# Expert blocks of a mixture-of-experts stage: projection ahead of the transposes, and a gather without a bound

## The reference

```
dest = pad_starts[sorted_e] + (arange(NK) - starts[sorted_e])   # NK = 2048 tokens * 2 experts each
row_tok = full((cap,), N).at[dest].set(flat_tok[order])          # padding rows point past the tokens
def expert_block(rows, e):                                       # 128 rows, one expert
    xb = t_pad[rows]                                             # 128 x 1024
    hid = silu(xb @ w_gate[e]) * (xb @ w_up[e])                  # 128 x 256
    return hid @ w_down[e]                                       # 128 x 1024
y = zeros((N + 1, D)).at[row_tok].add(y_rows * row_w)
```

## Time and profile before

| | us |
|---|---|
| median of 3 runs | 3779.98 |
| lowest and highest run | 3773.37, 3782.13 |
| the profiled execution, its own time | 3773.37 |
| its span, first to last instruction | 3771.6 |
| first gather of the expert stage | at 3156.08 |
| last scatter issued | at 3761.32 |

### The profile page before, as it was taken

One profiled execution on the slowest core, in us unless ns is written; L12 is line 12 of the kernel. 1 busy time (PEld: TensorE's weight loads), 2 busy tenths in 40 slices (PEclk: granted clock), 3 DMA queues, 4 the chain that ended last, 5 costly groups with the idle time before them and its releaser, 6 DMA issues. The chain is left out here.

```text
span 3771.6 us, 33286 instructions
## 1 busy us (share of the span) xinstructions
PE 3512.1 (93%) x11453; PEld 1842.2 (49%) x11453; DVE 1708.3 (45%) x4081; ACT 1037.4 (28%) x2543; POOL 986.2 (26%) x1362
## 2 busy tenths in 40 slices
PE   4999999999999899989999997999999996999998
PEld 3754455555445544434444444555565554444443
DVE  4656623443364573326665556543443543222222
ACT  3122222211100460002235445533322221222222
POOL 0277767400000681000000004655530000221221
PEclk8999999999999999999999998999999997999999
DMA  3134445434254002222221000000112224999997
GB/s 136 58 127 144 155 145 165 144 114 133 94 166 141 34 12 112 90 89 77 69 96 34 23 14 4 1 1 1 68 36 84 86 82 178 310 334 331 332 335 236
DMA packets 115563, 451.57 MB, mean 120 GB/s; under 512 B 15635, under 2 KB 43155, under 8 KB 103356
## 3 DMA queue, kind: packets, MB, share of 16 engines
q1 hardware_dynamic: 91484, 370.18, 27.6%
q0 software_dynamic: 18432, 58.74, 5.8%
q10 hardware_dynamic: 5472, 20.45, 1.5%
HBM read 340.28 MB, written 117.42 MB: 121 GB/s over the span
## 5 line engine op out<-in xcount | busy, mean ns | idle before, releaser
L142 PE MATMUL pst<-arena 128*128 128x512 f32 (+5 forms) x6938 | 2757.5, 555 | 68.9 <-DMA arena<-in_w_exp 28.2
L142 PEld LDWEIGHTS pst<-arena 128*128 128x128 f32 x6938 | 1301.5, 198 | 1368.5 <-issue 1260.0
L164 POOL TENSOR_TENSOR arena<-arena 128x4 f32<-128x4 f32 (+7 forms) x784 | 409.2, 522 | 464.0 <-DVE arena L2024 403.6
L164 DVE TENSOR_TENSOR arena<-arena 128x1 f32<-128x1 f32 (+8 forms) x1260 | 457.8, 364 | 95.4 <-ACT arena L2254 20.2
L147 PE MATMUL pst<-arena 128*128 128x128 f32 x2145 | 329.0, 288 | 141.9 <-DVE arena L246 52.4
L147 PEld LDWEIGHTS pst<-arena 128*128 128x128 f32 x2145 | 258.9, 147 | 324.2 <-issue 166.3
L1286 POOL TENSOR_SCALAR arena<-arena 128x384 f32<-128x384 f32 (+1 forms) x128 | 151.7, 1202 | 563.9 <-DVE arena L1278 563.9
L153 ACT ACTIVATE arena<-pst,arena 128x128 f32<-128x128 f32 (+1 forms) x630 | 243.9, 482 | 104.6 <-PE pst L147 102.1
L2201 POOL TENSOR_SCALAR arena<-arena 128x512 f32<-128x512 f32 (+3 forms) x160 | 218.3, 1383 | 174.9 <-DVE arena L164 158.6
L167 DVE TENSOR_SCALAR arena<-arena 128x1 f32<-128x1 f32 (+11 forms) x581 | 140.9, 242 | 190.1 <-DMA arena<-in_bc 78.5
L173 ACT ACTIVATE arena<-arena 128x1024 f32<-128x1024 f32 x48 | 50.7, 1057 | 628.0 <-DVE arena L1522 371.6
(11 more groups left out here) (194 smaller groups left out, 2112.5 us busy)
## 6 DMA issues: line engine op xcount, KB each, us to landing
arena<-in_w_exp SPq DMA_DIRECT2D x48, 3072.0 KB, 11.9
arena<-in_w_ada SPq DMA_DIRECT2D x48, 512.0 KB, 4.7
rotd<-arena POOLq DMA_DIRECT2D x32, 512.0 KB, 4.0
arena<-rotd SPq DMA_DIRECT2D x32, 512.0 KB, 4.5
arena<-sgd SPq DMA_DIRECT2D x16, 1024.0 KB, 7.7
arena<-pwd SPq DMA_DIRECT2D x32, 416.0 KB, 5.5
pwd<-arena SPq DMA_DIRECT2D x16, 576.0 KB, 5.9
h2d<-arena SPq DMA_DIRECT2D x17, 512.0 KB, 2.9
```

The source lines that it names most:

```text
L142: x = t.do.matmul(o, l, r, start=(i == 0), stop=(i == len(pairs) - 1))
L164: own(v, s).tensor_tensor(o, a, b, op).then_inc(*inc(s, *event))
```

## The change

Three edits, all in the expert stage.

1. The gather loses its bound, so every row is fetched, the padding rows too.
2. On TensorE `te_moe_up(b)` moves ahead of `te_moe_hidden(b - 1)`.
3. On VectorE `ve_moe_hidden` goes away and its copy becomes the first operation of `ve_moe_down`, so it moves behind `ve_moe_up(b)`.

```diff
@@ po_moe_gather @@
             p.do.indirect_dma_start(out=xr[b % 3], out_offset=None, in_=h2d,
-                                    in_offset=bass.IndirectOffsetOnAxis(ap=idT[:, b:b + 1], axis=0),
-                                    bounds_check=S - 1, oob_is_err=False
+                                    in_offset=bass.IndirectOffsetOnAxis(ap=idT[:, b:b + 1], axis=0)
                                     ).then_inc(*dma(f"moe_xr{b % 3}", "xr", b))
@@
-        def ve_moe_hidden(v, b):
+        def ve_moe_down(v, b):
+            q = "moe_ve"
             v.wait_ge(*at("moe_pe", "hT", b))
             v.wait_ge(*at("moe_pe", "down", b - 2, 1))
-            vcopy(v, hTt[b % 2].rearrange("p a b -> p (a b)"), bank(4)[:, 0:256]).then_inc(*inc("moe_ve", "hT", b))
-
-        def ve_moe_down(v, b):
-            q = "moe_ve"
+            vcopy(v, hTt[b % 2].rearrange("p a b -> p (a b)"), bank(4)[:, 0:256]).then_inc(*inc(q, "hT", b))
             y_stored(v, b - 2)
@@ te_moe_run @@
             for b in range(lo, hi + 1):
+                if b < hi:
+                    te_moe_up(t, b)
                 if b > lo:
                     te_moe_hidden(t, b - 1)
-                if b < hi:
-                    te_moe_up(t, b)
                 if b + 1 < hi:
                     te_moe_turn(t, b + 1)
@@ ve_moe_run @@
             for b in range(lo, hi + 1):
-                if b > lo:
-                    ve_moe_hidden(v, b - 1)
                 if b < hi:
                     ve_moe_up(v, b)
```

## The result

The changed kernel takes 3802.64 us, the median of five runs (3799.89 to 3806.53), against 3779.98 us before. The ratio is 1.0072, 95% interval 1.0051 to 1.0092, so it is slower by some 27 us by the ratio and by 23 us by the medians. One more execution of the changed kernel is on record, at 3817.81 us, above all of the five. The forecast was 3813 us in a range of 3794 to 3830. The profiled execution took 3799.97 us with a span of 3798.2, 26.6 us more than the span before.

The account below looks back on a forecast made before the run. Two bounds: a two-block loop of load latency plus `up` to `down`, 12.26 us a block, and TensorE's pace, 11.40. Terms 1.29 + 27.1 + 4.4 = 32.8 us, gather 0, gave 3812.8 on the median's scale, forecast 3813, range 3794 to 3830.

Parts of the forecast that it names:

- The copy behind the two multiplies delays each `down`: Expert stage, VectorE: the copy waits for tanh and two multiplies, so each `down` ends 1.29 us later after its `up`.
- The loop through the load is the pace, TensorE's own pace the floor: Expert stage: load-to-`down` loop over two blocks grows 23.99 to 25.28 us; TensorE's own pace 11.40 to 12.5 a block.
- The relief of loads that land sooner: Weight loads: landing down to 10.4 us in the longer period, loop stops binding; +14 us, 3794; chance 0.14.
- The wait for the copy: Sign in the steady stretch: TensorE waits for the L158 copy some 45 times, near 1.0 us each, 40 us or more.
- The half clock: Rival, TensorE: stalls plus weight waits slow `up` by 3 us in every third block; 48 us more, 3860; chance 0.03.
- The sum was 32.8 us: Whole expert stage: first `down` 1.29, 21 loop turns 27.1, three crossings and last block 4.4 us; loads unchanged.
- crossings: Places where the chain passes over a block whose `up` had its weights in time; each priced 1.1 us at TensorE's pace.
- 20 turns of the loop, without their loads: Load, `up`, `turn`, `down`, next load, spanning two blocks: each turn 1.29 us longer; the prediction priced 21 turns, 27.1 us.
- both ends of the stage: Expert stage's start and end: first `down` 1.29 us later, last block 1.1 us more at TensorE's pace, last loop turn 1.29.
- the upper bound of 8.9: Unbounded gather sharing engines with weight loads: at most 0.42 us for each of 21 loads of the loop, 8.9 us.
- The reason that was given: Unbounded gather: extra rows pass between two loads, and the period grows by about as much as they need; cost 0.
- The rival by the DMA share: Weight loads: share 0.97 read as full engines, extra gathered rows lengthen every load; +42 us, 3822; chance 0.15.

Follow-up runs that it names:

- the order alone: Changed kernel with the gather's bound put back (edits 2 and 3 alone): 3802.8 us, ratio 1.0074 to the kernel before; again, 3807.6 us, 1.0080.

## Why the prediction was right, and where its sizes were off

The mechanism of the reordering was right.

- *The copy behind the two multiplies delays each `down`.* Predicted 9.03 us from `up` to `down` and a loop of 25.28 us, of which 11.81 from the issue of the load to `up`. Measured 8.92 us, and 25.28 us with 11.91. The sum of the turn comes out exact because a shorter way to `down` and a slower load cancel in it. The experiments with one engine's order each show that VectorE's order is the cause and TensorE's costs at most a few microseconds.
- *The loop through the load is the pace, TensorE's own pace the floor.* Four buffers showed the floor at 12.35 us after; the prediction had 12.5. Before, its profile came to 11.61 us on the way to 11.40.
- *The relief of loads that land sooner* did not come: the landing stayed at 11.9 us.
- *The wait for the copy* was named as a sign with 1.0 us each and 40 us or more in all. It was 0.7 and 30.9. The prediction's own times give 3654.41 - 3653.6 = 0.8 and 36 us, so the sign was worked out wrongly, and the copy was 0.1 us earlier besides.
- *The half clock* played next to no part. The clock over the steady stretch was 1.00 against 0.99. One `up` each, 10.1 us before and 8.85 us after, both behind a late load, are all that the two chains show of it.

The sum was 32.8 us and the measurement is 23 to 27. Both chains run through 21 loads with three crossings, so the difference can be laid out. From first to last load the chain took 527.0 us before and 3742.43 - 3191.12 = 551.3 after, 24.3 more. For this piece the prediction had 20 x 1.29 + 3 x 1.1 = 29.1. The terms measured:

| term | predicted | measured |
|---|---|---|
| 20 turns of the loop, without their loads | 20 x 1.29 = 25.8 | 20 x 1.19 = 23.8 |
| 3 crossings | 3 x 1.1 = 3.3 | 3 x (12.35 - 11.40) = 2.9 |
| the 20 loads on the chain | 0 | 244.2 - 245.2 = -1.0 |
| `up` at half clock | 0 | 1.7 - 3.0 = -1.3 |

The rows behind the right column, from the chain of the kernel after (first load, the slow `up`, last load):

```profile
3191.12 11.62 DMA arena<-in_w_exp
...
3523.00 8.85 PE pst L142 x16
...
3742.43 11.96 DMA arena<-in_w_exp
```

So the term that was mis-sized is the delay of `down`, 1.29 us where 1.19 was measured, and in it the gap between the multiplies and the copy. The prediction took 0.03 us, as between tanh and multiply. The copy in fact began 0.09 us before the multiplies ended (3648.30 against 3648.39, in the rows of the section on the result). The gap that was taken lies between ScalarE and VectorE, this one within VectorE. The other two microseconds of the difference, from loads and clock, are those of a single profiled execution, and the forecast had no term for them. No run gives a reason for them, and a second profile of the changed kernel has a stage 7.4 us longer (607.1 against 599.7), so they are put down to chance. The rest of 32.8, 3.7 us for both ends of the stage, is below what the part ahead of the stage moves from one execution to the next.

Of the unbounded gather the prediction said 2048 rows, 8.4 MB, 20.4 us of engine time, and took 0 of it, because the period had grown by as much. In the old order the same rows cost 11 us (7 to 16 by the interval), around the upper bound of 8.9 that was given, with the landing at 12.4 us and with a part in the clock that the bound did not have. In the new order the timed runs agree with 0 and the profiles do not. The reason that was given is not shown: the landing of 11.9 us looks unchanged beside the kernel before, but the order alone has 11.8 and 11.9 where the changed kernel has 11.9 and 12.0, and no run placed the rows elsewhere. The rival by the DMA share (0.97 before, 0.96 after the earlier trace rows) forecast 42 us for the change as a whole, which did not come, and was right in kind for this edit alone. The Trainium skill ("DMA: Bandwidth & Descriptors", "Queues, rings and completion order") says that an engine takes turns between its queues, a packet from each. That the extra rows would therefore cost a load little was the prediction's inference and not the page's, and with edit 1 alone the landing rose by 0.5 us.

## What to carry to other kernels

When work moves within an engine that runs in order, ask what the moved instruction now stands behind, and follow that to the next engine and the next DMA. Here 0.4 us of copying landed behind a tanh and two multiplies that wait for TensorE. It delays each `down` by 1.2 us, and each block pays about half of that, since the loop spans two blocks. An edit's price can depend on the slack that the others leave: price it in the order in which it will run, and look in the profile for single long blocks before you put a mean down to a steady cost. And where a stage stands on two bounds this close, remove the latency (a fourth buffer) and the traffic (padding rows) together; the one without the other gave nothing, or half.

## What was not expected of the hardware

A full-looking DMA share says little: the engines showed 0.97 before and 0.94 with four buffers and the bounded scatter, where a block took 11.54 us against 12.23, with 43 scattered rows less in it. Four buffers alone ran at 1.00 and 344 GB/s in its profile, and its timed executions split in two groups 20 us apart. The views of these two kernels, windows from 3197 to 3700, four buffers first:

```profile
3197.00:3700.00 503.00, 493.31 (x1470) 239.48 (x1469) 113.33 (x217) 141.38 (x389) 112.93 (x86) 1.00 1.00 344
```

```profile
3197.00:3700.00 503.00, 497.78 (x1482) 242.92 (x1481) 113.33 (x217) 143.25 (x392) 114.00 (x87) 1.00 0.94 335
```

Dropping 2048 scattered rows, 42 us of engine time, gave 18 us in this loop (14 by the medians), and fetching 2048 more rows, 20.4 us of engine time, cost 11 us in the old order. The slowed `up` stood behind waits for weights of 1.9 us (changed kernel) to 3.4 us (edit 1 alone). Yet not every such wait slowed one: behind 2.5 us in the second profile of the changed kernel `up` took 7.13 us, and 45 waits of 0.7 us for the copy left the clock of the stretch at 1.00. The mean of a single profile holds such blocks or does not. A scattered row takes an engine 0.328 us, twice a gathered one. The row for it is GpSimd's queue in 3740.6 to 3741.4 of the kernel before, when only a scatter runs (packets, MB, share of 16 engines): 0.999 x 16 x 0.8 us over 39 packets.

```profile
q0 software_dynamic: 39, 0.16, 99.9%
```

GpSimd's gather instruction itself was 0.05 us shorter without its bound (0.989 against 1.041 us), which nothing waits for.
